# Row gates of the delta heads read through memory instead of rebuilt by matmuls, in a hybrid decoder block

## What is computed

```python
cum = jnp.cumsum(gate_chunks(g, c), axis=-1)
gamma = jnp.exp(jnp.where(causal_mask(c), cum[..., :, None] - cum[..., None, :], -jnp.inf))
kk = jnp.einsum('bhnid,bhnjd->bhnij', kc, kc)
a_mat = jnp.where(causal_mask(c, strict=True), beta[..., :, None] * kk * gamma, 0.0)
t_mat = a_mat + jnp.eye(c, dtype=f32)
u = lax.linalg.triangular_solve(t_mat, vc * beta[..., None], left_side=True, lower=True, unit_diagonal=True)
a_qk = jnp.einsum('bhnid,bhnjd->bhnij', qc, kc) * gamma
q_dec = qc * jnp.exp(cum)[..., None]
```

## Time and profile before

| | |
|---|---|
| median of 3 runs | 2774.84 us (2774.6 to 2779.07) |
| the profiled execution, its own time | 2773.6 us |
| its span, first to last instruction | 2771.6 us |
| mean granted clock of TensorE | 0.987 |
| PE busy | 96% of the span |
| DVE, ACT, POOL busy | 69%, 36%, 18% |
| chain of work that ended last | PE 70%, DVE 19%, ACT 8% |

### The profile page before, as it was taken

The page is one execution under the profiler, slowest core; times in us unless marked ns, Lnnn a source line. Parts: engine busy times, 40 slices in busy tenths (PEclk is TensorE's granted clock), DMA queues, the critical chain, the costliest instruction groups (busy, mean ns, idle before and its releaser), DMA issues.

```text
span 2771.6 us, 44953 instructions
## 1 busy us (share of the span) xinstructions
PE 2660.7 (96%) x16632; PEld 2343.6 (85%) x16632; DVE 1902.4 (69%) x3625; ACT 993.5 (36%) x2228; POOL 497.2 (18%) x433
## 2 busy tenths in 40 slices
PE   7999999999999999999999999998999999999998
PEld 3789789889888988988998898897878888888887
DVE  4677767867877776776776775776576666666656
ACT  4633643563374364345336325333430000000002
POOL 0000410310130031000000000000043443333440
PEclk9999999999999999999999999999999999999999
DMA  6221121122122112212212212223121111111111
GB/s 204 62 58 32 43 59 47 31 66 51 20 58 67 28 41 58 49 33 67 54 30 52 57 28 58 71 64 113 33 69 54 46 54 54 46 46 46 46 46 61
DMA packets 222618, 152.44 MB, mean 55 GB/s; under 512 B 27856, under 2 KB 207032, under 8 KB 222400
## 3 DMA queue, kind: packets, MB, share of 16 engines
q1 hardware_dynamic: 209728, 141.70, 17.7%
q0 software_dynamic: 12672, 7.87, 2.9%
HBM read 133.28 MB, written 16.26 MB: 54 GB/s over the span
## 4 chain that ended last, share of the span: by engine, by line
PE 70%; DVE 19%; ACT 8%; issue 2%; DMA 1%; SPq 0%; DVEq 0%; ACTq 0%
PE bank L179 27%; PE bank L171 17%; PE bank L2075 8%; DVE sig L1048 2%; PE bank L1194 2%; PE bank L1186 2%; PE bank L968 2%; DVE wB_lo L1101 1%; DVE wA_lo L1101 1%; PE bank L1141 1%; PE bank L443 1%; PE bank L1128 1%; DVE feat_region L1628 1%; DVE feat_region L1342 1%; PE bank L1516 1%
## 5 line engine op out<-in xcount | busy, mean ns | idle before, releaser
L171 PE MATMUL bank<-wB_hi,h_hi 128*128 128x256 f32 x1024 | 301.2, 294 | 4.4 <-ACT feat_region L1005 2.7
L171 PE MATMUL bank<-wA_hi,h_hi 128*128 128x256 f32 x1024 | 297.6, 291 | 4.6 <-ACT feat_region L1005 2.7
L171 PE MATMUL bank<-wB_lo,h_hi 128*128 128x256 f32 x1024 | 300.5, 293 | 0.0
L171 PE MATMUL bank<-wB_hi,h_lo 128*128 128x256 f32 x1024 | 300.1, 293 | 0.0
L171 PE MATMUL bank<-wA_lo,h_hi 128*128 128x256 f32 x1024 | 296.9, 290 | 0.0
L171 PE MATMUL bank<-wA_hi,h_lo 128*128 128x256 f32 x1024 | 296.8, 290 | 0.0
L179 PE MATMUL bank<-h_hi,wA_hi 128*128 128x512 f32 x672 | 267.4, 398 | 2.7 <-DVE feat_region L981 2.2
L179 PE MATMUL bank<-h_hi,wA_lo 128*128 128x512 f32 x672 | 267.5, 398 | 0.0
L179 PE MATMUL bank<-h_hi,wB_hi 128*128 128x512 f32 x672 | 267.4, 398 | 0.0
L179 PE MATMUL bank<-h_hi,wB_lo 128*128 128x512 f32 x672 | 267.3, 398 | 0.0
L179 PE MATMUL bank<-h_lo,wA_hi 128*128 128x512 f32 x672 | 266.5, 397 | 0.0
(11 more groups left out here) (395 smaller groups left out, 6232.9 us busy)
## 6 DMA issues: line engine op xcount, KB each, us to landing
w_raw<-in_w_in_dram SPq DMA_DIRECT2D x96, 512.0 KB, 3.8
w_raw<-in_w_ffn_up_dram SPq DMA_DIRECT2D x44, 512.0 KB, 3.8
rows_region<-in_ada_w_dram SPq DMA_DIRECT2D x64, 256.0 KB, 2.7
w_raw<-in_w_ffn_down_dram SPq DMA_DIRECT2D x22, 512.0 KB, 3.5
rows_region<-in_x_dram SPq DMA_DIRECT2D x8, 512.0 KB, 7.6
w_raw<-in_w_in_dram SPq DMA_DIRECT2D x16, 256.0 KB, 2.9
y_scratch<-ybuf SPq DMA_DIRECT2D x32, 128.0 KB, 1.9
y_scratch<-ybuf POOLq DMA_DIRECT2D x32, 128.0 KB, 3.1
```

The source lines that it names most:

```text
L171: mm = nc.tensor.matmul(bank[:, n_out:n_out + n1 - n0], (h_hi, h_lo)[hp][:, k, t * P:t * P + P], buf[wp][:, k, n0:n1], start=(s == 0), sto ...
```

## The change

1. **Row gates.** Part 1 of the front (L1141) goes, 4 matmuls for each of 32 pairs. In its place, once a head, PE transposes the 16 gate columns into 16 rows of `M[5]` (`rows_pe`, `r2` = 35, behind `gate_pre`). ACT copies them into `row_stage` (`rows_act`, the same beat). SP writes these 8 KB to `row_scratch` in device memory (`rows_sp`, beat 36, behind `gate_e`), waits for them to land, and reads tiles 0 to 3 back spread over all partitions, 512 KB into the half `conv_in[:, 1]` (beat 37). Tiles 4 to 7 follow at `r1` = 1 into `conv_in[:, 0]`. DVE's mask and ACT's `qdec` now read `conv_in` instead of bank `M[1]`. The gate columns are stored tile by tile (`g_row`), so that a half is one piece.
2. **Beats.** `LEVEL0` is 0, so a pair has 18 beats and `B1` is 72. DVE's `at`, the state's memset and the output of the last tile move behind the first L1331 of the pair. The front of pair 0 begins at `FRONT0` = 37, a beat earlier. `HEAD_AT`, `MOD_SUM_AT`, `ZERO_AT` and `STATE_AT` move with it.
3. **Tail.** The last two delta tiles put their output into `M[2]`, so that gathers in `M[5]` need not be kept from them; `GT_INNER` is 6, and tile 5 is gathered in `r1`. The buffer that holds the parts of `y` for the last round lies elsewhere in `conv_in`, and its loads also wait for `gdn_eq`. The last round's first scores wait for `gdn_y`.
4. A wait (`cols_read`) in the prologue goes; a load near the feed-forward part waits for `y_sum` too.

```diff
-                pe.wait_ge(sem("cols_read"), 1)
...
-    B1, B2, PAIR, CHUNK2, TAIL = 76, 42, 19, 5, 46
+    B1, B2, PAIR, CHUNK2, TAIL = 72, 42, 18, 5, 46
...
-    LEVEL0 = 1
+    LEVEL0 = 0
     TILE0 = LEVEL0 + 2 * len(LEVELS)
+    FRONT0 = B2 - 5
...
+    def rows_pe(pe, i, r):
+        if r == GATES_AT[i] + 2:
+            pe.wait_ge(sem("gate_pre"), i + 2)
+            nc.tensor.transpose(M[5][0:2 * NT, 256:256 + P], gq[:, 0:2].rearrange("p q t -> p (q t)"), ident[:]) \
+                .then_inc(sem("row_up"), 1)
+
+    def rows_act(act, step, i, r):
+        if r == GATES_AT[i] + 2:
+            act.wait_ge(sem("row_up"), i + 2)
+            step(nc.scalar.activation(row_stage, M[5][0:2 * NT, 256:256 + P], ACT.Copy))
+
+    def rows_load(sp, i, half):
+        name = f"row_in{half}"
+        if half == 0:
+            sp.wait_ge(sem("conv_ss"), 2 * (i + 1))
+        else:
+            sp.wait_ge(sem("conv_v"), i + 1)
+        o = GDN_TAPS - 1
+        sp.dma_start(conv_in[:, 1 - half, o:o + S],
+                     row_dram[NT * half:NT * half + NT].rearrange("a n -> (a n)").partition_broadcast(P)) \
+            .then_inc(sem(name), 16)
+
+    def rows_sp(sp, i, r):
+        if r == GATES_AT[i] + 3:
+            if i >= 0:
+                sp.wait_ge(sem("row_in0"), 32 * (i + 1))
+                sp.wait_ge(sem("row_in1"), 16 * (i + 1))
+            sp.wait_ge(sem("gate_e"), i + 2)
+            sp.dma_start(row_dram, row_stage).then_inc(sem("row_in0"), 16)
+        if r == GATES_AT[i] + 4:
+            sp.wait_ge(sem("row_in0"), 32 * (i + 1) + 16)
+            rows_load(sp, i + 1, 0)
...
-            for c in range(2):
-                for q in range(2):
-                    last = mm(M[1][:, (2 * c + q) * P:(2 * c + q + 1) * P],
-                              gq[:, q, 2 * d + c:2 * d + c + 1].broadcast_to([P, P]), ident[:], start=True,
-                              stop=True)
-            last.then_inc(sem("gdn_row"), 1)
...
-        dve.wait_ge(sem("gdn_row"), PAIRS * i + d + 1)
-        step(dve.tensor_tensor(wts[:].rearrange("p c (q t) -> p c q t", q=2),
-                               M[1][:].rearrange("p (c q t) -> p c q t", c=2, q=2),
+        dve.wait_ge(sem(f"row_in{d // 2}"), (32, 16)[d // 2] * (i + 1))
+        step(dve.tensor_tensor(wts[:].rearrange("p c (q t) -> p c q t", q=2), rows_of(d),
...
+    def out_bank(T):
+
+        return M[2 if T >= NT * N_IT - 2 else 5][:, 0:P]
...
+                if i == N_IT - 1:
+                    pe.wait_ge(sem("gdn_y"), NT * N_IT)
...
-    GT_INNER = 5
+    GT_INNER = 6
```

More of the change, by code:

```diff
@@ L549, in prologue_act @@
         step(A(vec_col, banks[5][:, 0:VEC], ACT.Copy))
-        step(A(conv_col[:], banks[4][:, 0:GDN_TAPS * 24], ACT.Copy), "cols_read")
+        step(A(conv_col[:], banks[4][:, 0:GDN_TAPS * 24], ACT.Copy))
         step(A(c_sig, c_col, ACT.Exp, scale=-1.0), "c_exp")
@@ L1130, in gdn_front_pe @@
             last.then_inc(sem("gdn_kq"), 1)
[L1131 to L1145 removed]
+        elif part == 2:
             if d == 0:
@@ L1237, in gdn_act @@
         elif j == 1:
-            act.wait_ge(sem("gdn_row"), D_ + 1)
-            step(A(qdec[:], M[1][:].rearrange("p (c q t) -> p c q t", c=2, q=2)[:, :, 1], ACT.Exp), "gdn_eq")
+            act.wait_ge(sem(f"row_in{d // 2}"), (32, 16)[d // 2] * (i + 1))
+            step(A(qdec[:], rows_of(d)[:, :, 1], ACT.Exp), "gdn_eq")
         elif j >= TILE0:
@@ L1251, in gdn_act @@
                     act.wait_ge(sem("g_y"), NT * i)
-                step(A(junk[:, 0:P], M[5][:, 0:P], ACT.Square, accum_out=rs[:, 0:1]))
+                step(A(junk[:, 0:P], out_bank(T), ACT.Square, accum_out=rs[:, 0:1]))
                 step(A(rs[:, 1:2], rs[:, 0:1], ACT.Ln, scale=1.0 / GDN_DV, bias=eps[:]))
@@ L1599, in chunk_dve @@
                 dve.wait_ge(sem("part_in"), 16 * (6 if c < 6 else NT))
-                step(tt(ybuf[:, c % 2], ybuf[:, c % 2], y_part[:, c], ALU.add), "y_sum")
+                step(tt(ybuf[:, c % 2], ybuf[:, c % 2], y_part(c), ALU.add), "y_sum")
     CONV_AT = {}
@@ L2149, in _ @@
                     mod_sp(sp, i, r1)
+                    if r1 == 1:
+                        rows_load(sp, i, 1)
+                elif r2 is not None and i < N_IT - 1:
+                    rows_sp(sp, i, r2)
                 if r1 == 0 and branch(i) == "gla":
```

84 lines of the change are left out of this document (44 added, 40 removed).

## The result

The changed kernel takes **2779.76 us** (median of 19 runs, 2773.76 to 2783.86) against 2774.62 us of the kernel before in the same session (19 runs). The ratio is 1.0015, with a 95% interval of 1.0008 to 1.0022. I had forecast 2763.7 us, faster. The time is 16.1 us above the forecast and outside its range: the change makes the kernel no faster, and if anything slightly slower.

The account below looks back on a forecast made before the run. PE, busy 96% of the span, was the bound: its work plus its waits. -28.8 + 1.8 + 13.6 + 6.2 - 3.9 = -11.1 us from 2773.6 gave 2762.5, as median 2763.7 us; 8-in-10 range 2751 to 2774 us.

Parts of the forecast that it names:

- row matmuls removed: PE's four row matmuls per group: 0.90 us saved for each of 32 groups, 28.8 us in all.
- new transposes: PE's transpose of the gate columns: 0.23 us, 8 times, 1.8 us added; bounds 0.5 and 3 us.
- wait for the gates: PE at beat 35 waits for DVE's last gate column: 13.6 us added, bounds 8 and 20 us.
- boundary of the rounds: Pair 0's first level waits for the solve: 0.4 us or 1.4 us a round, 6.2 us added, bounds 2 and 10.
- pairs of 18 beats: Solve levels in shorter pairs: longer beats and one lost beat cancel, 0 us; bounds -5 and +8 us.
- tail: Tile gathers at the end: waits of 2.49 and 1.45 us go, 3.32 us stays; 3.9 us less.
- other waits: PE waits outside the listed steps: no term in the sum; cols_read, y_sum and gdn_eq called behind later events.
- clock: Rival: idle at beat 35 lowers PE's clock, 5.1 us an episode; chance 0.15 for one or two, 0.07 for four or more.
- DVE becomes the bound within pairs: Rival: one more 0.53 us wait at each of 24 starts of pairs 1 to 3, 12.8 us; 2776.5 us, chance 0.12.
- Round 5's 4.11 us: Round 5's share of PE's forecast wait at beat 35 for the gate column: 4.11 us, against 2.60 in round 4.
- The copy through memory: Store and load of the gate rows on SP: some 6.3 us, covered before the mask needs them, so nothing added.

Follow-up runs that it names:

- e7: Kernel before with each group of four row matmuls issued twice; 2801.77 us, ratio 1.0097 to before.
- e2: Changed kernel with the beat change undone except FRONT0 (19-beat pairs, LEVEL0 = 1, DVE's moved operations back at beat 0); 2760.32 us.
- e1: Changed kernel with pairs of 19 beats again, LEVEL0 = 0 and DVE's moved operations kept; 2796.37 us.
- e5: e2 with at, the memset and the last tile's output left behind the first level's product, as in the changed kernel; 2761.44 us.
- e6: Changed kernel with DVE's output gates and the second half of each weight split one beat later; 2751.35 us.
- e9: Changed kernel with only the output gates (ZG_AT) one beat later; 2769.09 us.
- e3: Changed kernel with the gates' transpose, ACT's copy, the store and the load each one beat later; 2769.70 us.
- e8: e4 with tile 7's load issued three beats earlier into a free buffer and x of tile 4 loaded three beats later; 2753.69 us.
- e10: Kernel before with only the second half of each weight split 3 beats behind the first instead of 2; 2772.83 us.
- e11: e4 with the second half of each weight split 3 beats behind the first instead of 2; 2749.25 us.
- e12: e6 with the transpose of the gates one beat later, as in e3; 2749.35 us.
- e4: Changed kernel with e2's undone beat change and e3's gate transpose one beat later; 2751.07 us, ratio 0.9909 to before.

## Why the prediction was wrong, step by step

In profiled spans I forecast -11.1 us and got +7.9 us, a difference of 19.0 us.

| step | forecast | measured | from |
|---|---|---|---|
| row matmuls removed | -28.8 | -25.1 | busy time of e7 |
| new transposes | +1.8 | +1.8, taken over | not measured by itself |
| wait for the gates | +13.6 | +11.9 | wait L1134 |
| boundary of the rounds | +6.2 | +7.2 | wait L1224 <- L1327 |
| pairs of 18 beats | 0 (-5 to +8) | +15.4 | +21.3, -4.9, -1.0: waits for L1378, for the level's product, L1248 |
| tail | -3.9 | -0.9 | 9.1 against 10.0 us of waits for split and load |
| other waits | 0 | -4.9 | the rest of PE's idle time, 28.7 - 33.6 |
| clock | 0 | +2.5 | what is left of busy time: -20.8, against -25.1 + 1.8 |

**The step that failed** is the one on pairs of 18 beats, "I let gain and loss cancel; the bounds are -5 and +8 us". Its working asked how long a beat is and how many beats lie between the solve and the first level. It never asked what else DVE does in the beats where the levels now stand. The table in the section on waits shows the answer: +15.4 us of waits where I had put 0. e2 puts the price at 19.4 us with the boundary, some 12 us without its wait of 7.2, and e1 and e5 show that neither the shorter pair nor the moved operations bring it. It was the start of the levels on beat 0, where they meet DVE's other work: shown by e6 and e9 for pair 0, read from the timeline for pairs 1 and 3. The clock, which I had also put at nothing, is a second and smaller term, 2.5 us here. The direction was among the rivals, as "DVE becomes the bound within pairs", 2776.5 us with a chance of 0.12; but its mechanism, one more wait at each of 24 starts, is not what happened. Levels 1 to 3 wait, and pair 0, which has no such start, with 8.8 us nearly as much as pair 1 with 10.1. That its time came nearer than my sum is luck. I had given the two facts that decide it, a DVE "busy without a gap there" and the fixed beats of its other work, in the wrong place: as a remark for and against a rival, not as a row to be read.

**The gates** were right: 11.9 us in 8 places, 0.96 to 1.32 us in the GLA rounds, 2.48, 2.49 and 1.99 in the mLSTM rounds. Round 5's 4.11 us, which I had taken for a property of that round, comes and goes: such a wait of 4.0 us stands in round 6 in e1 and e9, in round 4 in e5, and nowhere in e2. The lead's 0.71 us I had left out. e3 shows the price to be the wait.

**The boundary** was right, with 0.69 and 1.25 us for 0.4 and 1.4. e2 takes it away.

**The tail** was mis-sized. The waits of 2.49 and 1.45 us went as I said, and a wait of 3.32 us for the load of tile 7 took their place; the wait of 3.32 us that I had kept is 2.30 us. I had read who waits for the split on DVE, not when the load is issued. e8 shows that under this load wait stands the split again. This edit of the loads alone does not shorten the tail.

**The copy through memory** at nothing was right: one wait of 2.8 us in the lead, and no more. That the operand's place, PSUM or SBUF, changes nothing for this size holds on all 32 masks: 691 ns before, 692 now. The difference of 62 cycles between the two sources, which follows from the figures of the Trainium skill in "VectorE: DVE Perf Modes", section on the TRN2 errata, doesn't show in this operation.

**The clock.** My rival said that new waits at beat 35 bring half-speed stretches. In the changed kernel they don't. These are 10 us each of the changed kernel, behind the waits for the gates in rounds 0, 4, 5 and 6, and behind the mLSTM wait of 3.4 to 3.7 us in rounds 4 and 5 (the third number from the end is the granted clock):

```profile
370.30:380.30 10.00, 9.97 (x81) 9.47 (x82) 3.84 (x6) 3.06 (x8) 0.86 (x1) 1.00 0.55 172
...
1293.60:1303.60 10.00, 10.00 (x77) 9.68 (x78) 4.74 (x12) 3.38 (x10) 0.85 (x1) 1.00 0.58 173
1519.00:1529.00 10.00, 10.00 (x65) 9.68 (x65) 3.61 (x7) 2.81 (x7) 0.85 (x1) 0.83 0.58 171
1746.70:1756.70 10.00, 10.00 (x77) 9.68 (x78) 4.74 (x12) 3.37 (x10) 0.85 (x1) 1.00 0.55 173
1259.70:1269.70 10.00, 9.55 (x36) 8.26 (x37) 3.47 (x9) 6.47 (x12) 0.85 (x1) 0.56 0.31 67
1485.20:1495.20 10.00, 9.76 (x36) 8.29 (x37) 3.48 (x9) 6.73 (x12) 0.85 (x1) 0.55 0.31 67
```

Only one of the seven waits for the gates in the rounds is followed by anything, 0.83 over 10 us, 1.7 us lost. In e2, though, 0.83 follows all three of its gate waits of 2.5 us. The waits of 3.4 us and more are followed by 0.56 and 0.55 (and 0.53 in round 6), 4.4 to 4.7 us lost each. Three such waits, of 3.38 and 3.39 us, stood in the kernel before as well. The first two of them are followed by

```profile
1257.50:1267.50 10.00, 9.43 (x54) 8.52 (x55) 4.35 (x12) 7.72 (x14) 0.84 (x1) 0.83 0.32 66
1478.70:1488.70 10.00, 9.97 (x37) 8.82 (x38) 3.49 (x9) 6.50 (x12) 0.86 (x1) 0.54 0.32 66
```

and the third by 0.55. So the same wait can end either way. In e9, whose three mLSTM waits are those of the changed kernel to 0.02 us, the clock behind them is 0.83, 0.84 and 0.54: 5.7 us less lost, with no difference in these waits. In e6 this wait is 1.8 to 2.2 us in each of the three rounds, and the 10 us behind it read

```profile
1240.00:1250.00 10.00, 10.00 (x60) 9.15 (x61) 5.74 (x15) 8.42 (x15) 1.29 (x2) 0.84 0.33 68
1461.80:1471.80 10.00, 9.43 (x67) 8.62 (x68) 6.51 (x15) 8.54 (x15) 1.31 (x2) 1.00 0.34 67
1683.40:1693.40 10.00, 9.96 (x59) 9.13 (x60) 5.67 (x15) 8.30 (x15) 1.17 (x2) 0.83 0.32 66
```

Over all fourteen profiled executions the picture is the same. In ten kernels the three mLSTM rounds have this wait at 3.4 to 3.7 us, and the 10 us behind it have a clock of 0.51 to 0.57 in 19 of 30 places and 0.83 to 0.85 in 11. In the four kernels with the splits moved (e6, e10, e11, e12) it is 1.8 to 2.2 us, and they have 0.83 or 0.84 in 6 of 12 places and 1.00 in 6; half speed follows none. With it the mean clock of the timed runs goes up from 0.986 to 0.989 (before to e10) and from 0.985 to 0.988 (e4 to e11), by the move of the splits alone. The shorter wait is the likely way, though this move changes other waits too. It is not all: e9 rises from 0.984 to 0.986 and leaves this wait at 17.1 us in all, and e12 falls from 0.990 to 0.987 with fewer waits than e6. What else moves the clock stays open.

## What to carry to other kernels

When a step on a critical chain of small operations is moved by a beat, lay it beside everything else that its engines do in the new beats. An engine that is busy for 69% can be full in exactly the beat that counts, and then order within its queue, not work, sets the price. Here one beat cost some 12 us. Moving the chain back gave it back whole. Moving the other work gave back 9 us of these waits, and as much again elsewhere. When a wait is taken away, look for what is next in the same place, the load as well as the engine. And price an edit whose gain is a sum of many small pieces by doubling the piece.
